# Two passes instead of three for two narrow projections of a hybrid encoder step

## The chip, the cores and the metric

The kernel runs on one core of a Trainium2 chip. The metric is the device time of one execution in microseconds, as the median of several runs. The engines are named as in the profile: PE multiplies matrices, PEld is its weight loading, ACT, DVE and POOL are the three engines that work on elements, and SP issues the DMA transfers.

## The reference, cut to what matters

The program is one inference step of a trunk with two layers, for 1,024 prompt frames and 32 sample frames that share the weights. Each layer normalises its input, projects it, mixes, and projects back. Two of the projected parts are very narrow: the step sizes `dt_raw` of the first layer (16 columns, one for each head) and the forget logits `f_logit` of the second (8 columns).

```python
h = rmsnorm(x, g_pre)
proj = jnp.einsum('bld,de->ble', h, w_in)
u, v, za, zb, xbc, dt_raw = jnp.split(proj, EVEN_SPLITS, axis=-1)   # even layer
dt = jax.nn.softplus(dt_raw.astype(jnp.float32) + dt_bias.astype(jnp.float32))
...
q, k, v, z, f_logit = jnp.split(proj, ODD_SPLITS, axis=-1)          # odd layer
logf = jax.nn.log_sigmoid(f_logit.astype(jnp.float32))
f_cum = jnp.cumsum(jnp.concatenate([past_logf.astype(jnp.float32), logf], axis=1), axis=1)
```

## The kernel before

All 1,056 frames (`TOK`) are handled together, in three chunks of 352 columns (`CH`). The normalised input stands turned in SBUF, features in the partitions, in eight slices of 128 (`k`), and as two numbers for each element: a rounded high part `HH` and the rest `HL`. A weight tile is 128 output columns wide. SP loads it into `WRAW` (two slots, taken in turn), ACT copies it with rounding into `WH` (`split_high`), and POOL subtracts to get the rest `WL` (`split_low`). PE then makes three products for each slice and chunk, high by high, low by high and high by low, into one bank, `PB[c]`: 24 multiplications for a chunk, 72 for a tile. ACT reads each chunk out.

The order on every engine is written out by hand and semaphores tie the engines together. `w_high` and `w_low` count the tiles that ACT and POOL have split; SP may load the next tile into a slot once `w_low` says that the old one was split; `c_read0` to `c_read2` count the chunks that ACT has read out of a bank; `p_chunk` counts chunks that PE has finished.

The tile numbers name the places that matter here. `W_BC[0]` (0) and `W_DT` (1) are the first two tiles; PE works on them in turns (`first_step`), with the turning of `XS` into `HH` and `HL` between them (`x_turn`, three turnings for each slice, through a ring of three banks that ACT and DVE empty). `W_DT` has only 16 real columns, and the other 112 are zeros. Then come `W_BC[1]` to `W_BC[3]`. Behind chunk 0 of `W_BC[1]`, nine turnings bring `DTRAW` (the step sizes) into the frames' order, and DVE and ACT compute on them until PE needs `DTA` for the running sums.

At the border of the two layers the order on PE is: `W_F` (93, 8 real columns) chunks 0 and 1, then chunk 0 of the value tile V, the turning of the sample rows, of row tile 6, chunk 1 of V, the turning of row tile 7, chunk 2 of `W_F`, chunk 2 of V, the nine turnings of `FRAW` (the logits), and chunk 0 of the gate tile Z. A running sum over the logits (`INC`, by a scan on DVE) must be there before PE goes on (`sum_forget`). SP's loads stand in one line: `W_F`, V, Z, then the rows `XT` of tile 7 again, and behind `h1_lo` (17 counts: the second layer's input is complete) the cached logits and the tiles Q and K.

Of the kernel before, what the change touches and what calls it, by code (L numbers as in the profile page):

```python
# [101 lines left out]
def hybrid_trunk(nc, x_prompt, x_sample, cache_k, cache_v, cache_logf, state_ssd, state_conv,  # L102
# [103 lines left out]
    r = Region(A_R5 + 4 * TOK * 4, A_W)  # L206
    DTRAW = r("DTRAW", [HEADS_B, 9 * P])
    DTX, DTN, DTE, DTW, DTL, DTC, DTA, DTD = [r(f"DT{n}", [P, 9, HEADS_B]) for n in "XNEWLCAD"]
# [70 lines left out]
    r = Region(A_R5 + 4 * TOK * 4, A_W)  # L279
    FRAW = r("FRAW", [HEADS_C, 9 * P])  # L280
    FX, FN, FE, FW, FL, FC = [r(f"F{n}", [P, 9, HEADS_C]) for n in ("X", "N", "E", "W", "L", "C")]
# [337 lines left out]
    def _(pool):  # L619
        order = Order(pool, S("pool_order"))  # L620

        def split_low(w):
            pool.wait_ge(S("w_high"), times(w, 1, 1))
            if not isinstance(w[2], int) or w[0] + w[1] * w[2] >= 2:
                pool.wait_ge(S("p_chunk"), times(w, 3, -3))
            pool.tensor_tensor(WL[:, slot(w), :, :], WRAW[:, slot(w), :, :], WH[:, slot(w), :, :].bitcast(f32),  # L626
                               ALU.subtract).then_inc(S("w_low"), 1)

        def split_lows(ws):
            for w in ws:  # L630
                split_low(w)
# [12 lines left out]
        for w in range(W_XZ + 4):  # L644
            split_low(tile_no(w, 1, 0))

# [28 lines left out]
        for u in range(2, OE_UNITS):  # L675
# [3 lines left out]
                               WHS[SLOT3[u % 3]][:, HALF:D].bitcast(f32), ALU.subtract).then_inc(S("w_low"), 1)  # L679
        split_low(tile_no(W_F, 1, 0))  # L680
        split_low(tile_no(W_QKVZ + V_, 4, 0))
# [75 lines left out]
    def _(pe):  # L757
# [11 lines left out]

        def project_chunk(w, u, c, hi, lo, start=True, stop=True, ready=None, ks=range(KT)):  # L770

            if c == 0:
                pe.wait_ge(S("w_low"), times(w, 1, 1))
            if start and not (isinstance(u[2], int) and u[0] + u[1] * u[2] == 0):
                pe.wait_ge(S(f"c_read{c}"), times(u, 1, 0))
            cols = slice(c * CH, (c + 1) * CH)
            for k in ks:
                if ready and len(ready) == 2:
                    pe.wait_ge(S(ready[k % 2]), c * 4 + k // 2 + 1)
                elif ready and (c == 0 or len(ks) < KT):  # L780
                    pe.wait_ge(S(ready[0]), k + 1)
                wh, wl = WH[:, slot(w), k, :], WL[:, slot(w), k, :]
                mm(PB[c][:, 0:CH], wh, hi[:, k, cols], start=start and k == 0, stop=False)
                mm(PB[c][:, 0:CH], wh, lo[:, k, cols], start=False, stop=False)
                last = mm(PB[c][:, 0:CH], wl, hi[:, k, cols], start=False, stop=stop and k == KT - 1)
            if ks[-1] == KT - 1:
                last.then_inc(S("p_chunk"), 1)
# [27 lines left out]
        def first_step(w, c, bank, k):  # L815

            if k == 0:
                pe.wait_ge(S("w_low"), w + 1)
            pe.wait_ge(S("h_lo"), c * KT + k + 1)
            cols = slice(c * CH, (c + 1) * CH)  # L820
            mm(PB[bank][:, 0:CH], WH[:, w, k, :], HH[:, k, cols], start=k == 0, stop=False)
            mm(PB[bank][:, 0:CH], WH[:, w, k, :], HL[:, k, cols], start=False, stop=False)
            last = mm(PB[bank][:, 0:CH], WL[:, w, k, :], HH[:, k, cols], start=False, stop=k == KT - 1)
            if k == KT - 1:
                last.then_inc(S("p_chunk"), 1)
# [28 lines left out]
        for b in range(NB + 1):  # L854
            last = turn(PB[3][:, b * HEADS_B:(b + 1) * HEADS_B], DTRAW[:, b * P:(b + 1) * P])
        last.then_inc(S("dt_turn"), 1)
# [240 lines left out]
        pe.wait_ge(S("h1_lo"), 12)  # L1097
        project_chunk(w_f, u_f, 0, HH, HL)
        project_chunk(w_f, u_f, 1, HH, HL)
        project_chunk(w_v, u_v, 0, HH, HL)  # L1100
# [7 lines left out]
        pe.wait_ge(S("h1_lo"), 17)  # L1108
        project_chunk(w_f, u_f, 2, HH, HL)
        def turn_forget():  # L1110

            pe.wait_ge(S("fc"), 1)
            pe.wait_ge(S("c_read2"), W_F - OE_UNITS + 1)
            for b in range(NB + 1):
                last = turn(PB[3][:, b * HEADS_C:(b + 1) * HEADS_C], FRAW[:, b * P:(b + 1) * P])
            last.then_inc(S("lt_turn"), 1)
# [214 lines left out]
    def _(act):  # L1331
# [106 lines left out]

        raw = whole(DTRAW, HEADS_B)
        for c in range(3):  # L1440
            read_first(c, parted(XR, 3, SAMP), c, 2 * c + 1)
            if c == 2:
                act.wait_ge(S("w_raw0"), loads_of_slot(tile_no(W_BC[1], 1, 0)))
                copy(WH[:, 0, :, :], WRAW[:, 0, :, :]).then_inc(S("w_high"), 1)
            read_first((7, 6, 5)[c], raw, c, 2 * c + 2, HEADS_B)
        split_high(tile_no(W_BC[2], 1, 0))
# [271 lines left out]
        def read_f(c):  # L1718
            act.wait_ge(S("p_chunk"), 3 * W_F + (1, 2, 5)[c])
            copy(FRAW[:, c * CH:(c + 1) * CH], PB[c][0:HEADS_C, 0:CH]).then_inc(S(f"c_read{c}"), 1)  # L1720

# [198 lines left out]
    def _(dve):  # L1920
# [653 lines left out]
```

## Time and profile before

| what | us |
|---|---|
| median of 3 runs (lowest, highest) | 1576.73 (1575.45, 1576.91) |
| time of the profiled execution | 1575.49 |
| its span, first to last instruction | 1573.8 |
| PE busy | 1534.6 (98%) |
| DVE, ACT, POOL busy | 794.0, 677.1, 444.7 |

### The profile page before, as it was taken

The page shows a single profiled execution, that of the slowest core. Times are in us where ns is not written, and L with a number is a line of the kernel's source. Part 1 is how long each engine was busy: PE and PEld are TensorE (multiplying, and loading weights), DVE is VectorE, ACT ScalarE, POOL GpSimd, SP SyncE. Part 2 cuts the span into 40 slices and gives each one's busy share as a digit, 9 for nine tenths or more (in the row PEclk, how much of TensorE's full clock was granted, in tenths as well). Part 3 has the DMA queues.
Part 4 walks back from the last instruction along what each step waited for, and adds up shares of the span by engine and source line. Part 5 has one row for each costly group of instructions (what it writes and reads, how often), then busy time and mean ns, then how long its engine had stood idle before and what let it go on. Part 6 is the DMA issues. An engine that isn't in the chain of part 4 may idle for free.

```text
span 1573.8 us, 26349 instructions
## 1 busy us (share of the span) xinstructions
PE 1534.6 (98%) x9472; PEld 1415.8 (90%) x9472; DVE 794.0 (50%) x1751; ACT 677.1 (43%) x1258; POOL 444.7 (28%) x268
## 2 busy tenths in 40 slices
PE   6999999999999999999999999999999999999998
PEld 5999999999999999988888898999999999988776
DVE  5546777676884231436475243444344343435432
ACT  6444443433233322335455344445454545455321
POOL 1214453553221111344343221222222231215000
PEclk9999999999999999999999999999999999999999
DMA  5122223213102111254456536614241423213121
GB/s 154 43 70 61 74 62 101 60 45 86 53 27 57 41 40 40 79 175 160 153 192 145 56 75 53 68 37 74 37 71 44 71 41 63 61 44 141 55 98 70
DMA packets 129510, 121.09 MB, mean 77 GB/s; under 512 B 10290, under 2 KB 113292, under 8 KB 129452
## 3 DMA queue, kind: packets, MB, share of 16 engines
q1 hardware_dynamic: 129452, 120.32, 31.5%
q8 instruction: 37, 0.61, 0.2%
q14 instruction: 21, 0.17, 0.0%
HBM read 101.64 MB, written 18.66 MB: 76 GB/s over the span
## 4 chain that ended last, share of the span: by engine, by line
PE 88%; ACT 4%; DVE 3%; issue 3%; DMA 1%; POOL 1%; SPq 0%; ACTq 0%; DVEq 0%; POOLq 0%
PE PB L759 83%; PE PB L763 5%; DMA XT<-in_x_prompt_dram 1%; ACT L1339 1%; ACT L1804 1%; ACT SB L1893 0%; ACT SQJ L1373 0%; DVE XT L1931 0%; DMA WOR<-in_w_out_odd_dram 0%; DVE SB L1928 0%; ACT WH L1333 0%; POOL WL L626 0%; DMA XS<-in_x_prompt_dram 0%; DVE XS L1928 0%; DVE M L1931 0%
## 5 line engine op out<-in xcount | busy, mean ns | idle before, releaser
L759 PE MATMUL PB<-HH,WH 128*128 128x352 f32 x1872 | 617.5, 330 | 2.5 <-DVE HL L1924 1.6
L759 PE MATMUL PB<-HH,WL 128*128 128x352 f32 x1872 | 601.9, 322 | 0.0
L759 PE MATMUL PB<-HL,WH 128*128 128x352 f32 x1872 | 601.1, 321 | 0.0
L759 PEld LDWEIGHTS PB<-HH,WH 128*128 128x128 f32 x1872 | 351.9, 188 | 17.5 <-issue 10.4
L759 PEld LDWEIGHTS PB<-HL,WH 128*128 128x128 f32 x1872 | 352.9, 189 | 0.2
L759 PEld LDWEIGHTS PB<-HH,WL 128*128 128x128 f32 x1872 | 351.9, 188 | 0.0
L626 POOL TENSOR_TENSOR WL<-WRAW,WH 128x1024 fp32r<-128x1024 f32 x81 | 199.9, 2468 | 534.3 <-ACT WH L1333 527.6
L1333 ACT ACTIVATE WH<-WRAW 128x1024 fp32r<-128x1024 f32 x112 | 118.0, 1054 | 14.3 <-DMA WRAW<-in_w_out_even_dram 6.1
L1893 ACT ACTIVATE SB<-SB,small 128x128 f32<-128x128 f32 (+8 forms) x72 | 53.8, 748 | 78.6 <-DVE small L1928 78.6
L1924 DVE TENSOR_TENSOR Y<-PB,Y 128x128 f32 (+3 forms) x72 | 20.2, 281 | 127.6 <-PE PB L759 127.5
L759 PE MATMUL PB<-PT,VTOK 128*128 128x128 f32 (+2 forms) x624 | 81.5, 274 | 0.0
L759 PEld LDWEIGHTS PB<-PT,VTOK 128*128 128x128 f32 (+1 forms) x624 | 78.3, 191 | 1.5
L759 PE MATMUL PB<-KALL,QT 128*128 128x512 f32 (+4 forms) x208 | 78.0, 482 | 0.0
L654 POOL TENSOR_TENSOR M<-M,CBT 128x512 f32<-128x512 f32 (+1 forms) x48 | 62.2, 1324 | 47.5 <-ACT M L1522 47.5
L759 PE MATMUL PB<-WH,YSH 128*128 128x512 f32 x192 | 75.1, 391 | 0.0
L759 PE MATMUL PB<-WL,YSH 128*128 128x512 f32 x192 | 74.7, 389 | 0.0
L1333 ACT ACTIVATE PT<-PB 128x512 f32<-128x512 f32 (+3 forms) x112 | 45.9, 447 | 61.2 <-PE PB L763 61.1
L678 POOL TENSOR_TENSOR WL<-WRAW,WH 128x512 fp32r<-128x512 f32 x30 | 53.5, 1784 | 63.6 <-ACT WH L1333 63.6
L759 PE MATMUL PB<-WH,YSL 128*128 128x512 f32 x172 | 66.9, 389 | 0.0
L1924 DVE TENSOR_TENSOR UG<-UG,ZG 128x1056 f32<-128x1056 f32 x8 | 12.2, 1528 | 105.6 <-ACT ZG L1353 105.6
L2442 DVE CUSTOM_DVE_ANT_0 SB<-PB,NFB 128x512 f32<-128x512 f32 (+4 forms) x104 | 54.5, 547 | 21.4 <-issue 14.4
L704 POOL TENSOR_TENSOR NRM<-QT 128x352 f32<-128x352 f32 x24 | 20.0, 832 | 147.9 <-ACT QT L1333 147.9
(312 smaller groups left out, 2362.6 us busy)
## 6 DMA issues: line engine op xcount, KB each, us to landing
WRAW<-in_w_out_even_dram SPq DMA_DIRECT2D x48, 512.0 KB, 3.6
WRAW<-in_w_in_even_dram SPq DMA_DIRECT2D x44, 512.0 KB, 3.8
WRAW<-in_w_in_odd_dram SPq DMA_DIRECT2D x32, 512.0 KB, 8.2
ACSB<-acs_rows SPq DMA_DIRECT2D x16, 528.0 KB, 5.3
NFB<-nf_rows SPq DMA_DIRECT2D x8, 656.0 KB, 3.9
XS<-in_x_prompt_dram SPq DMA_DIRECT2D x8, 512.0 KB, 6.2
XT<-in_x_prompt_dram SPq DMA_DIRECT2D x8, 512.0 KB, 5.3
x_rows<-OG SPq DMA_DIRECT2D x8, 512.0 KB, 5.4
```

The lines of the kernel that those rows point to most:

```text
L626: pool.tensor_tensor(WL[:, slot(w), :, :], WRAW[:, slot(w), :, :], WH[:, slot(w), :, :].bitcast(f32), ALU.subtract).then_inc(S("w_low"), 1)
L654: pool.tensor_tensor(m, m, CBT[0:rows, g, b0:b0 + nb, 0:rows], ALU.mult).then_inc(S("m"), 1)
L678: pool.tensor_tensor(WLS[SLOT3[u % 3]][:, HALF:D], raw[:, HALF:D], WHS[SLOT3[u % 3]][:, HALF:D].bitcast(f32), ALU.subtract).then_inc(S("w_ ...
L704: last = pool.tensor_tensor(NRM[:, n, cols], src, src, ALU.mult)
L759: return pe.matmul(out, lhsT, rhs, start=start, stop=stop)
L763: return pe.transpose(out, in_, IDENT[0:n, 0:n])
L1333: return act.activation(out, in_, ACT.Copy, scale=scale)
L1339: act.add_instruction(mybir.InstLoadActFuncSet(name=nc.get_next_instruction_name(), act_func_set_id=LN_EXP_SET, ins=[], outs=[]))
L1804: act.activation(Y1[:, p, :], Y1[:, p, :], ACT.Silu).then_inc(S("zs"), 1)
L1893: act.activation(SB[0:rows, 0:width], SB[0:rows, 0:width], ACT.Exp, scale=SCALE, bias=NBIAS[0:rows, :], accum_out=RSUM[0:rows, :]).then_in ...
L1924: return dve.tensor_tensor(out, a, b, op)
L2442: order(dve.tensor_tensor_reduce(SB[0:rows, c0:c1], PB[3 + k][0:rows, 0:c1 - c0], NFB[0:rows, key0 + c0:key0 + c1], 1.0, -3.0e38, ALU.add, ...
```

## The change

In the two narrow tiles the low parts of the weights are put into the columns beside the high ones: columns 16 to 31 of `WH` for `W_DT`, columns 8 to 15 for `W_F` (`stack_low` on POOL, for 128 and 64 elements of each partition, in place of 1,024). PE then needs two passes, with `HH` and with `HL`, and not a third with `WL`. The projection comes out with twice the rows, the high weights' part above the low weights' part, and ACT copies 32 or 16 rows. The two halves are added when they are turned: in place of a turning against the identity, PE multiplies with `STACKB` or `STACKC`, two identities on top of each other, which DVE makes once.

```diff
+        def stack_low(w, heads):
+            pool.wait_ge(S("w_high"), times(w, 1, 1))
+            pool.tensor_tensor(WH[:, slot(w), :, heads:2 * heads], WRAW[:, slot(w), :, 0:heads],
+                               WH[:, slot(w), :, 0:heads].bitcast(f32), ALU.subtract).then_inc(S("w_low"), 1)
...
         for w in range(W_XZ + 4):
-            split_low(tile_no(w, 1, 0))
+            if w == W_DT:
+                stack_low(tile_no(w, 1, 0), HEADS_B)
+            else:
+                split_low(tile_no(w, 1, 0))
...
-        split_low(tile_no(W_F, 1, 0))
+        stack_low(tile_no(W_F, 1, 0), HEADS_C)
         split_low(tile_no(W_QKVZ + V_, 4, 0))
...
                 mm(PB[c][:, 0:CH], wh, hi[:, k, cols], start=start and k == 0, stop=False)
-                mm(PB[c][:, 0:CH], wh, lo[:, k, cols], start=False, stop=False)
-                last = mm(PB[c][:, 0:CH], wl, hi[:, k, cols], start=False, stop=stop and k == KT - 1)
+                end = stop and k == KT - 1
+                last = mm(PB[c][:, 0:CH], wh, lo[:, k, cols], start=False, stop=stacked and end)
+                if not stacked:
+                    last = mm(PB[c][:, 0:CH], wl, hi[:, k, cols], start=False, stop=end)
...
-            last = mm(PB[bank][:, 0:CH], WL[:, w, k, :], HH[:, k, cols], start=False, stop=k == KT - 1)
+            if w != W_DT:
+                last = mm(PB[bank][:, 0:CH], WL[:, w, k, :], HH[:, k, cols], start=False, stop=k == KT - 1)
...
-            last = turn(PB[3][:, b * HEADS_B:(b + 1) * HEADS_B], DTRAW[:, b * P:(b + 1) * P])
+            last = mm(PB[3][:, b * HEADS_B:(b + 1) * HEADS_B], DTRAW[:, b * P:(b + 1) * P], STACKB[:, :])
...
-                last = turn(PB[3][:, b * HEADS_C:(b + 1) * HEADS_C], FRAW[:, b * P:(b + 1) * P])
+                last = mm(PB[3][:, b * HEADS_C:(b + 1) * HEADS_C], FRAW[:, b * P:(b + 1) * P], STACKC[:, :])
...
+        for stack, heads in ((STACKB, HEADS_B), (STACKC, HEADS_C)):
+            order(tt(stack[:, :], IDENT[0:2 * heads, 0:heads], IDENT[0:2 * heads, heads:2 * heads], ALU.add))
+        order.fence()
         dve.memset(DTRAW[:, TOK:], 0.0).then_inc(S("dtc"), 1)
```

On PE, the end of chunk 2 of `W_DT` and the first multiplications of `W_BC[1]` read like this before:

```order
L759 MATMUL PB<-HH,WH 128x352 [waits h_lo]
L759 MATMUL PB<-HL,WH 128x352
L759 MATMUL PB<-HH,WL 128x352
L759 MATMUL PB<-HH,WH 128x352 [waits h_lo]
L759 MATMUL PB<-HL,WH 128x352
L759 MATMUL PB<-HH,WL 128x352
L759 MATMUL PB<-HH,WH 128x352 [waits c_read0,w_low]
L759 MATMUL PB<-HL,WH 128x352
```

and like this in the changed kernel:

```order
L769 MATMUL PB<-HH,WH 128x352 [waits h_lo]
L769 MATMUL PB<-HL,WH 128x352
L769 MATMUL PB<-HH,WH 128x352 [waits h_lo]
L769 MATMUL PB<-HL,WH 128x352
L769 MATMUL PB<-HH,WH 128x352 [waits h_lo]
L769 MATMUL PB<-HL,WH 128x352
L769 MATMUL PB<-HH,WH 128x352 [waits c_read0,w_low]
L769 MATMUL PB<-HL,WH 128x352
L769 MATMUL PB<-HH,WL 128x352
```

Each slice of `W_DT` has lost its third multiplication, and the wait for `w_low` of `W_BC[1]` now stands behind 16 multiplications of the chunk and not 24.

On PE, the place where `DTRAW` is turned, behind chunk 0 of `W_BC[1]`, reads like this before:

```order
L759 MATMUL PB<-HL,WH 128x352
L759 MATMUL PB<-HH,WL 128x352
L763 MATMUL PB<-IDENT,DTRAW 128x16 [waits dtc,c_read2]
L763 MATMUL PB<-IDENT,DTRAW 128x16 x8
L759 MATMUL PB<-HH,WH 128x352 [waits c_read1]
```

and like this in the changed kernel:

```order
L769 MATMUL PB<-HL,WH 128x352
L769 MATMUL PB<-HH,WL 128x352
L769 MATMUL PB<-STACKB,DTRAW 128x16 [waits dtc,c_read2]
L769 MATMUL PB<-STACKB,DTRAW 128x16 x8
L769 MATMUL PB<-HH,WH 128x352 [waits c_read1]
```

Nothing has moved, but the nine turnings are plain products of 32-bit numbers. The nine of `FRAW` change in the same way.

On POOL, the splits at the border of the layers (`WLC` is the last tile of the first layer's output projection, then follow `W_F` and V) read like this before:

```order
L678 TENSOR_TENSOR WLC<-WRAW,WHC 128x512 [waits w_high]
L626 TENSOR_TENSOR WL<-WRAW,WH 128x1024 [waits p_chunk,w_high] x2
L683 CAST IDENTB<-IDENT 128x128 [waits h1_lo]
L684 MEMSET MASKD 128x128
L687 AFFINE_SELECT MASKD<-MASKD 128x128 [waits pool_order]
```

and like this in the changed kernel:

```order
L688 TENSOR_TENSOR WLC<-WRAW,WHC 128x512 [waits w_high]
L633 TENSOR_TENSOR WH<-WRAW,WH 128x8x8 [waits w_high]
L628 TENSOR_TENSOR WL<-WRAW,WH 128x1024 [waits p_chunk,w_high]
L693 CAST IDENTB<-IDENT 128x128 [waits h1_lo]
L694 MEMSET MASKD 128x128
```

The split of `W_F` is smaller and no longer waits for `p_chunk`, that is, for PE to have finished with the slot of `WL`. SP's load of tile Z, which waits for `w_low` of `W_F`, and the load of `XT` behind it can go out earlier.

## Rows read from the trace of the kernel before

**Rows 1.** The page, the chain that ended last, shares by engine.

```profile
PE 88%; ACT 4%; DVE 3%; issue 3%; DMA 1%; POOL 1%; SPq 0%; ACTq 0%; DVEq 0%; POOLq 0%
```

**Rows 2.** Timeline of PE: first, last multiplication of chunk 2 of `W_DT`, then `W_BC[1]`.

```profile
start us, us, engine line op out<-in xcount [idle before <-releaser]
...
49.56 0.32 PE L759 MATMUL PB<-HH,WH 128*128 128x352 f32 x1
...
53.22 0.32 PE L759 MATMUL PB<-HH,WL 128*128 128x352 f32 x1
53.79 0.43 PE L759 MATMUL PB<-HH,WH 128*128 128x352 f32 x1 [0.25 <-POOL WL L626]
```

**Rows 3.** Timeline of PE: first, fourth turning beside `W_DT` chunk 0; first beside `W_BC[0]` chunk 1.

```profile
27.55 0.49 PE L763 MATMUL PB<-IDENT,XS 128*128 128x128 f32 x3
...
30.55 0.55 PE L763 MATMUL PB<-IDENT,XS 128*128 128x128 f32 x3 [0.39 <-DVE HL L1931]
...
35.24 0.55 PE L763 MATMUL PB<-IDENT,XS 128*128 128x128 f32 x3
```

**Rows 4.** Timeline of DVE: the last normalised rows, those of the sample.

```profile
33.91 0.74 DVE L1928 TENSOR_SCALAR XS<-XS,small 32x1024 f32<-32x1024 f32 x1
```

**Rows 5.** Timeline of ACT: first read behind chunk 2 of `W_BC[0]`.

```profile
49.76 0.53 ACT L1333 ACTIVATE XR<-PB 128x320 f32<-128x320 f32 x2 [3.36 <-PE PB L759]
```

**Rows 6.** Timeline of PE: the nine turnings of `DTRAW` and what follows them.

```profile
57.85 0.73 PE L763 MATMUL PB<-IDENT,DTRAW 16*128 16x16 f32 x9
58.50 0.43 PE L759 MATMUL PB<-HH,WH 128*128 128x352 f32 x1
```

**Rows 7.** Timeline of PE: `sum_forget`, two and four small products, and what follows.

```profile
887.38 0.43 PE L759 MATMUL PB<-LT,TRIF 128*128 128x88 f32 x2 [1.63 <-DVE INC L2393]
887.64 0.55 PE L759 MATMUL PB<-INC,ONES 128*128 128x56 f32 x4
888.04 0.41 PE L759 MATMUL PB<-HH,WH 128*128 128x352 f32 x1
```

**Rows 8.** Timelines of DVE and PE: `DTA`, and the running sums over it.

```profile
65.95 0.31 DVE L1924 TENSOR_TENSOR DTA<-TOKQ,EALB 128x144 f32<-128x144 f32 x1
...
66.32 0.51 PE L759 MATMUL PB<-DTA,TRI 128*128 128x144 f32 x2
```

**Rows 9.** Timelines of ACT, POOL and PE: V is split, and its chunk 0 starts.

```profile
854.65 1.05 ACT L1333 ACTIVATE WH<-WRAW 128x1024 fp32r<-128x1024 f32 x1
...
855.77 3.39 POOL L626 TENSOR_TENSOR WL<-WRAW,WH 128x1024 fp32r<-128x1024 f32 x1 [4.51 <-ACT WH L1333]
...
859.22 0.43 PE L759 MATMUL PB<-HH,WH 128*128 128x352 f32 x1
```

**Rows 10.** The chain that ended last: rows `XT` of tile 7, issue to landing.

```profile
851.71 9.84 DMA XT<-in_x_prompt_dram
```

**Rows 11.** Timelines of PE and ACT: tile 6 turned, `FRAW` chunk 1 read, chunk 1 of V.

```profile
864.92 1.06 PE L763 MATMUL PB<-IDENT,XT 128*128 128x128 f32 x8 [1.00 <-DVE XT L1931]
...
865.27 0.44 ACT L1333 ACTIVATE FRAW<-PB 8x352 f32<-8x352 f32 x1
...
865.76 0.43 PE L759 MATMUL PB<-HH,WH 128*128 128x352 f32 x1
```

**Rows 12.** Timelines of PE and SP: chunk 2 of `W_F`; Q's load issued, and its time to landing.

```profile
872.29 0.43 PE L759 MATMUL PB<-HH,WH 128*128 128x352 f32 x1 [1.57 <-DVE HL L1924]
...
872.69 0.47 SPq L367 DMA_DIRECT2D WRAW<-in_w_in_odd_dram  x1
...
DMA to landing us min/median/max: 8.7/8.7/8.7
```

**Rows 13.** Timelines of ACT, POOL and DVE: Q is split, and `FW` of the logits.

```profile
881.49 1.05 ACT L1333 ACTIVATE WH<-WRAW 128x1024 fp32r<-128x1024 f32 x1
...
882.61 2.38 POOL L626 TENSOR_TENSOR WL<-WRAW,WH 128x1024 fp32r<-128x1024 f32 x1 [2.32 <-ACT WH L1333]
...
882.84 2.21 DVE L1928 TENSOR_SCALAR FW<-FE 128x72 f32<-128x72 f32 x1 [0.33 <-ACT FE L1839]
```

**Rows 14.** Issue of V's load (842.2) and its time to landing.

```profile
DMA to landing us min/median/max: 7.7/7.7/7.7
```

More of the change, by code:

```diff
@@ L159, in hybrid_trunk @@
     DCOL = const("DCOL", [P, 8])
+    STACKB = const("STACKB", [2 * HEADS_B, HEADS_B])
+    STACKC = const("STACKC", [2 * HEADS_C, HEADS_C])
     small = const("small", [P, 64])
@@ L206, in hybrid_trunk @@
     r = Region(A_R5 + 4 * TOK * 4, A_W)
-    DTRAW = r("DTRAW", [HEADS_B, 9 * P])
+    DTRAW = r("DTRAW", [2 * HEADS_B, 9 * P])
     DTX, DTN, DTE, DTW, DTL, DTC, DTA, DTD = [r(f"DT{n}", [P, 9, HEADS_B]) for n in "XNEWLCAD"]
@@ L279, in hybrid_trunk @@
     r = Region(A_R5 + 4 * TOK * 4, A_W)
-    FRAW = r("FRAW", [HEADS_C, 9 * P])
+    FRAW = r("FRAW", [2 * HEADS_C, 9 * P])
     FX, FN, FE, FW, FL, FC = [r(f"F{n}", [P, 9, HEADS_C]) for n in ("X", "N", "E", "W", "L", "C")]
@@ L768, in key_wait, with project_chunk @@
                 pe.wait_ge(S("masks"), 1)
-        def project_chunk(w, u, c, hi, lo, start=True, stop=True, ready=None, ks=range(KT)):
+        def project_chunk(w, u, c, hi, lo, start=True, stop=True, ready=None, ks=range(KT),
+                          stacked=False):
             if c == 0:
@@ L821, in first_step @@
             mm(PB[bank][:, 0:CH], WH[:, w, k, :], HH[:, k, cols], start=k == 0, stop=False)
-            mm(PB[bank][:, 0:CH], WH[:, w, k, :], HL[:, k, cols], start=False, stop=False)
-            last = mm(PB[bank][:, 0:CH], WL[:, w, k, :], HH[:, k, cols], start=False, stop=k == KT - 1)
+            last = mm(PB[bank][:, 0:CH], WH[:, w, k, :], HL[:, k, cols], start=False,
+                      stop=w == W_DT and k == KT - 1)
+            if w != W_DT:
+                last = mm(PB[bank][:, 0:CH], WL[:, w, k, :], HH[:, k, cols], start=False, stop=k == KT - 1)
             if k == KT - 1:
@@ L1097, in _ @@
         pe.wait_ge(S("h1_lo"), 12)
-        project_chunk(w_f, u_f, 0, HH, HL)
-        project_chunk(w_f, u_f, 1, HH, HL)
+        project_chunk(w_f, u_f, 0, HH, HL, stacked=True)
+        project_chunk(w_f, u_f, 1, HH, HL, stacked=True)
         project_chunk(w_v, u_v, 0, HH, HL)
@@ L1108, in _ @@
         pe.wait_ge(S("h1_lo"), 17)
-        project_chunk(w_f, u_f, 2, HH, HL)
+        project_chunk(w_f, u_f, 2, HH, HL, stacked=True)
         def turn_forget():
@@ L1437, in read_first @@
             last.then_inc(S(f"c_read{c}"), 1)
-        raw = whole(DTRAW, HEADS_B)
+        raw = whole(DTRAW, 2 * HEADS_B)
         for c in range(3):
@@ L1444, in _ @@
                 copy(WH[:, 0, :, :], WRAW[:, 0, :, :]).then_inc(S("w_high"), 1)
-            read_first((7, 6, 5)[c], raw, c, 2 * c + 2, HEADS_B)
+            read_first((7, 6, 5)[c], raw, c, 2 * c + 2, 2 * HEADS_B)
         split_high(tile_no(W_BC[2], 1, 0))
@@ L1719, in read_f @@
             act.wait_ge(S("p_chunk"), 3 * W_F + (1, 2, 5)[c])
-            copy(FRAW[:, c * CH:(c + 1) * CH], PB[c][0:HEADS_C, 0:CH]).then_inc(S(f"c_read{c}"), 1)
+            copy(FRAW[:, c * CH:(c + 1) * CH], PB[c][0:2 * HEADS_C, 0:CH]).then_inc(S(f"c_read{c}"), 1)
         squares(SMP)
```

## The prediction

> **What bounds the kernel now.** I read the page first, then the chain that ended last, then the timelines of the two places that the change touches. The page gives PE 88% of the chain [rows 1], so PE's own work is the time nearly everywhere, and a multiplication taken off PE is worth its pace as long as PE doesn't wait next for something that has not become earlier. The pace: 24 multiplications of a chunk start from 49.56 to 53.22 [rows 2], 3.66 us for 23 steps, 0.159 us each. The change removes 48 of them, 24 in each layer, so 7.63 us is the most there is. The timelines then show where PE, just behind each removed piece, stands or would stand waiting for POOL, ACT, DVE or a transfer. That decides the sum, so I go through both places in order of time. Beyond them PE has hardly a gap and the loads are released by its own progress, so I carry an earlier start through to the end.
>
> **First place, W_DT.** The change there, piece by piece:
>
> Chunk 0. The first four slices are mixed with turnings. The fourth group of turnings starts at 30.55, after a wait of 0.39 us for DVE's `HL` [rows 3]. That wait goes back to a turning before 27.55 and to ACT and DVE work behind it, which holds no multiplication of `W_DT`. So the three removed before 30.55 only lengthen the wait: nothing. Five remain (slices 3 to 7): 5 x 0.159 = 0.80 us. The next turnings then are ready at 35.24 - 0.80 = 34.44, but they need the sample rows, which DVE ends at 33.91 + 0.74 = 34.65 [rows 3, 4]. With the 0.05 us from such an end to PE's start, 34.70: the gain is 0.54 us.
>
> Chunk 1. No wait is recorded in it, and DVE's ring has room: 8 x 0.159 = 1.27 us. Sum 1.81 us.
>
> Chunk 2. Here is the first loss. `W_BC[1]` can't start before its weights are split, and that split begins only when chunk 2 of `W_BC[0]` is done: ACT reads that chunk at 49.76, rounds the tile, POOL subtracts, and PE starts at 53.79 having waited 0.25 us for POOL [rows 2, 5]. All of this moves by 1.81 us with the chunk that starts it, to 51.98. Chunk 2 of `W_DT` is what PE does meanwhile. It gets 8 x 0.159 = 1.27 us shorter, and PE waits 1.27 us longer. Gain still 1.81 us.
>
> The turning. Nine turnings take 58.50 - 57.85 = 0.65 us [rows 6]. A plain product of 32-bit numbers shows as two instructions. Six small ones take 888.04 - 887.38 = 0.66 us, 0.11 each [rows 7]. Nine products are 18 instructions, 1.98 us, 1.33 us more than before. The ends: at the turnings' own pace (0.65 / 9 = 0.072) 18 cost 1.30 us, 0.65 more; at the most that the wider pair of the running sums leaves (0.51 us for two with their tail [rows 8]) 18 cost 4.6 us, 3.9 more. I take 0.11, since those rows are as narrow. Would it be hidden? PE reaches the running sums at 66.32 just when `DTA` is there (65.95 + 0.31 = 66.26 [rows 8]). `DTA` hangs on the convolution that begins with the read of rows 5, so it moves 1.81 us, and PE arrives later than it: nothing hides the 1.33 us. First place: 1.81 - 1.33 = 0.48 us gained, between 1.16 gained and 2.1 lost.
>
> The Trainium skill speaks against this step twice. "Perfetto Trace Analysis", section Transposes, wants a transposition done as one and not as an ordinary product, and rows 6 and 7 have that sign. "TensorE: Matmul & The Clock Gate", section LDWEIGHTS, prices a weight load by its columns alone, 128 columns over 1.2, or 107 ns; by it my estimate would be 18 x 0.107 = 1.93 us, and the sum would gain 0.05 us. The turnings load 128 columns too and pass at 0.072 us, so as a rule for every load it doesn't hold here.
>
> The rest is free. The two additions for the stacks and the larger clear stand on DVE between the last `HL` and the convolution, where it is idle until the read of rows 5. ACT's copies have twice the partitions and the same columns. POOL's smaller split is not waited for by PE.
>
> **Second place, W_F.** Chunks 0 and 1 lose 16 multiplications, 2.54 us. But V's chunk 0 starts at 859.22, and POOL's split of V ends at 855.77 + 3.39 = 859.16; that split begins when ACT, after squares of rows and a root chain, rounds V at 854.65 [rows 9]. None of it waits for `W_F`'s products. PE waits 2.5 us in their place. Gain 0.
>
> Then SP. `w_low` of `W_F` came at about 851.3 and let SP issue Z and, behind it, `XT`, which landed 9.84 us after 851.71 and held the chain [rows 10]. Now POOL's small split waits only for ACT's rounding, and `XT` can be issued and lands some us earlier. PE's wait of 1.00 us before tile 6 is turned goes away [rows 11]. But V's chunk 1 also needs its bank, and ACT reads `FRAW` out of that bank only at 865.27 + 0.44 = 865.71, behind the squares of row tile 7 and behind the sample rows, which PE turns after V's chunk 0; PE starts chunk 1 at 865.76, 0.05 us later [rows 11]. So two releases tie, and removing one gives nothing: gain 0, with 1.0 us as the bound if I misread the tie.
>
> Chunk 2 of `W_F` starts at 872.29 when `h1_lo` is complete [rows 12], unmoved, and is 8 x 0.159 = 1.27 us shorter. V's chunk 2 and the turnings follow that much earlier. What then holds PE is `INC`, for which it waits 1.63 us until 887.38 [rows 7]. `INC` hangs on `FW`, which DVE holds for 2.21 us, until 882.84 + 2.21 = 885.05, just when POOL ends its split of Q at 882.61 + 2.38 = 884.99. POOL starts after ACT rounds Q at 881.49 [rows 13]. And ACT can't do that before Q has landed: 872.69 + 8.7 = 881.4 [rows 12]. Q's load waits for `h1_lo`, unmoved. So `INC` stays, and the 1.27 us turn into waiting. The nine dearer products of `FRAW` (1.33 us) fit into the 1.63 + 1.27 us of wait. Second place: 0.
>
> **Sum.** 0.48 + 0 = 0.5 us. The profiled execution took 1575.49 us (span 1573.8 and 1.7 around it) and would take 1575.0. The median of the runs shown is 1576.73, 1.24 us above it, so 1576.2. About 0.2%, 3.2 us, is what a measurement of this kernel can tell from no change; this is far inside it. Most of the 7.63 us of removed PE work becomes waiting: 0.48 + 0.26 in chunk 0, 1.27 in chunk 2, 3.81 at the border.
>
> **Rivals.**
>
> (a) The border does open. If the bank's read is not what holds V's chunk 1, the 1.00 us comes through, `h1_lo` and Q's load move by it, and `INC` with them. With the cheaper end of the turning (0.65 instead of 1.33) the gain is 0.48 + 1.0 + 0.68 = 2.2 us: 1574.5. For it: the recorded wait is put down to DVE alone. Against it: 865.71 and 865.76.
>
> (b) The work simply goes: PE's share of 88% as it stands. 48 x 0.159 - 2 x 1.33 = 5.0 us, 1571.7. It needs all four waits to be something else than I read them. Against it: each ends within 0.1 us of PE's start.
>
> (c) Slower: V comes late. Z and `XT` now go out while V's load is on its way (issued 842.2, 7.7 us to landing, so 849.9 [rows 14]). If the transfers shared the engines, V could land as the last of the three, later by up to the 9.84 us that Z and `XT` took together [rows 10]: 859.7. ACT wants V at 854.65 [rows 9]; that is the point from which it costs. 859.7 - 854.65 = 5.1 us, less 0.5: 1581.3, slower by 0.3%. Against it: rows in one queue that I read land in the order of their issue.
>
> (d) The stacked turning is at its dear end, 3.9 us more at the first place: 1576.7 + 2.1 = 1578.8. At the second place the excess of about 1 us over the waits would come on top if the logits got late.
>
> **How the numbers follow.** Forecast (between 1.5 us gained and 1.5 lost) 0.66; (a) 0.16; (b) 0.08; (c) 0.05; (d) 0.05. Faster by over 0.2% takes (b) and a little of (a): 0.09. Slower takes half of (c) and a little of (d): 0.04. The rest, 0.87, is the same. The range leaves out (b) and (c): from (a), less 0.7 us, half the spread of the three runs shown, 1573.8, to 1578.3, short of (d).
>
> **What the changed profile would show.** PE waits about 1.5 us for POOL before `W_BC[1]`, which starts near 52.0; 18 instructions on `STACKB` in about 2.0 us; the running sums near 65.8. PE waits about 2.5 us before V's chunk 0 at 859.2 less 0.5 (the carried gain), and `XT` no longer stands in the chain. Before `sum_forget` PE waits some 1.6 us or more. I am wrong if V's chunk 1 comes much earlier than ACT's second read of `FRAW` did, if `FW` is not held by POOL, or if a product with the stack costs over 0.3 us.

## The result: 7.5 us slower, and most of it in code that the change doesn't touch

The changed kernel takes 1583.26 us (5 runs, 1582.13 to 1584.09) against 1575.81 us of the kernel before (5 runs, 1575.19 to 1576.91): ratio 1.0043, 95% interval 1.0032 to 1.0054. I had forecast 1576.2 and a range up to 1578.3. The profiled execution has a span of 1581.3 us, 7.5 us more than before.

The page's row for PE, with the counts of its instructions:

```profile
PE 1539.0 (97%) x9442; PEld 1414.7 (89%) x9442; DVE 788.4 (50%) x1753; ACT 677.3 (43%) x1258; POOL 440.8 (28%) x268
```

PE has 30 instructions fewer than before (48 multiplications gone, 9 turnings replaced by 18 instructions at each of two places), and yet is busy for 1539.0 us where it was 1534.6. So this is not waiting alone: work that is left has become slower.

Where the 7.5 us come from is read from the starts of the same piece of work in the two traces:

| piece of work | before | after | difference |
|---|---|---|---|
| `W_BC[1]` chunk 0 starts [rows 2] | 53.79 | 51.87 | -1.92 |
| first multiplication behind the nine turnings [rows 6] | 58.50 | 58.03 | -0.47 |
| running sums over `DTA` [rows 8] | 66.3 | 67.4 | +1.1 |
| output projection of the first layer, first multiplication | 655.43 | 656.26 | +0.83 |
| the same, last multiplication | 851.05 | 857.31 | +6.26 |
| V chunk 0 [rows 9] | 859.22 | 865.27 | +6.05 |
| `sum_forget` [rows 7] | 887.38 | 893.51 | +6.13 |
| the turning of `NFT` behind it | 891.98 | 899.66 | +7.68 |
| span | 1573.8 | 1581.3 | +7.5 |

Three steps stand out: 5.4 us in the output projection, and twice 1.5 us just behind a place of the change (58 to 67 us, and 893 to 900 us). I call such a difference between the two traces, in the start of the same piece of work, the drift.

**First place.** Timeline of PE in the changed kernel: the start of `W_BC[1]`, the products with `STACKB`, and what follows them.

```profile
start us, us, engine line op out<-in xcount [idle before <-releaser]
51.87 0.43 PE L769 MATMUL PB<-HH,WH 128*128 128x352 f32 x1 [1.48 <-POOL WL L628]
...
55.93 2.18 PE L769 MATMUL PB<-STACKB,DTRAW 32*128 32x16 f32 x18
58.03 0.43 PE L769 MATMUL PB<-HH,WH 128*128 128x352 f32 x1
58.30 0.41 PE L769 MATMUL PB<-HL,WH 128*128 128x352 f32 x1
58.50 0.49 PE L769 MATMUL PB<-HH,WL 128*128 128x352 f32 x1
58.80 0.49 PE L769 MATMUL PB<-HH,WH 128*128 128x352 f32 x1
...
61.44 0.49 PE L769 MATMUL PB<-HH,WH 128*128 128x352 f32 x1
61.73 0.36 PE L769 MATMUL PB<-HL,WH 128*128 128x352 f32 x1
```

The wait of 1.5 us for POOL and the start at 51.87 are as forecast. The eighteen product instructions hold PE for 58.03 - 55.93 = 2.10 us. Behind them the multiplications start 0.29 us apart instead of 0.159, for 3.4 us. The windows give the granted clock (the column behind POOL, 1.00 being 2.4 GHz; a stretch wholly at 1.2 GHz shows 0.50); the kernel before has 1.00 in all of these:

```profile
core 0: us, PE busy (x) PEld busy (x) DVE busy (x) ACT busy (x) POOL busy (x), PEclk, DMA share, GB/s
58.00:60.00 2.00, 2.00 (x9) 1.97 (x10) 0.00 (x0) 1.98 (x3) 0.00 (x0) 0.60 0.19 57
60.00:62.00 2.00, 2.00 (x9) 2.00 (x9) 1.10 (x6) 1.08 (x4) 0.00 (x0) 0.55 0.00 0
62.00:64.00 2.00, 2.00 (x14) 2.00 (x13) 1.66 (x6) 0.91 (x3) 0.00 (x0) 1.00 0.00 0
...
895.00:900.00 5.00, 5.00 (x25) 4.96 (x24) 0.00 (x0) 0.14 (x1) 0.00 (x0) 0.69 0.40 43
```

**Output projection.** Timeline of PE in the middle of this stage, two rows 27 multiplications apart:

```profile
699.60 0.40 PE L769 MATMUL PB<-WL,YSH 128*128 128x512 f32 x1
...
705.92 0.39 PE L769 MATMUL PB<-WLC,YSHD 128*128 128x512 f32 x1
```

That is 6.32 / 27 = 0.234 us each. In the kernel before, two rows of the same stage, again 27 multiplications apart, give 6.12 / 27 = 0.227 us each:

```profile
699.76 0.39 PE L759 MATMUL PB<-WH,YSH 128*128 128x512 f32 x1
...
705.88 0.39 PE L759 MATMUL PB<-WH,YSH 128*128 128x512 f32 x1
```

No wait is recorded and the clock is 1.00 in both. The groups by form say the same, with the duration of one in ns behind the comma. The kernel before, then the changed one:

```profile
L759 PE MATMUL PB<-WH,YSH 128*128 128x512 f32 x180 | 70.3, 391 | 0.0
...
L759 PE MATMUL PB<-WHC,YSHD 128*128 128x512 f32 x90 | 35.3, 392 | 0.0
```

```profile
L769 PE MATMUL PB<-WH,YSH 128*128 128x512 f32 x179 | 71.2, 398 | 0.0
...
L769 PE MATMUL PB<-WHC,YSHD 128*128 128x512 f32 x84 | 33.6, 400 | 0.0
```

**Border.** Timelines of POOL, PE and DVE from `W_F` to `sum_forget`:

```profile
851.44 0.32 POOL L633 TENSOR_TENSOR WH<-WRAW,WH 128x64 fp32r<-128x64 f32 x1 [3.42 <-ACT WH L1348]
...
865.27 0.43 PE L769 MATMUL PB<-HH,WH 128*128 128x352 f32 x1 [2.44 <-POOL WL L628]
871.84 0.43 PE L769 MATMUL PB<-HH,WH 128*128 128x352 f32 x1 [0.82 <-ACT FRAW L1348]
878.37 0.43 PE L769 MATMUL PB<-HH,WH 128*128 128x352 f32 x1 [1.57 <-DVE HL L1939]
...
885.86 2.17 PE L769 MATMUL PB<-STACKC,FRAW 16*128 16x8 f32 x18
...
889.14 2.05 DVE L1943 TENSOR_SCALAR FW<-FE 128x72 f32<-128x72 f32 x1 [0.33 <-ACT FE L1854]
...
893.51 0.43 PE L769 MATMUL PB<-LT,TRIF 128*128 128x88 f32 x2 [1.47 <-DVE INC L2411]
```

Here nearly every wait is the one forecast: 2.44 us for POOL's `WL` before V's chunk 0; before V's chunk 1 no longer DVE's `XT` but 0.82 us for ACT's read of `FRAW`, the second of the two tied releases; `FW` at the end of POOL's split, and the wait for `INC`. The drift is the same before and behind these waits.

### The profile page after: what moved, and what is told of

Same layout as the page of the kernel before. It is cut to its first block and busy times, and to the rows that moved or that the text cites. A ratio compares the mean times of both kernels' runs of the same rounds, so it can differ in the third digit from the quotient of the medians.

```text
span 1581.3 us, 26290 instructions
## 1 busy us (share of the span) xinstructions
PE 1539.0 (97%) x9442; PEld 1414.7 (89%) x9442; DVE 788.4 (50%) x1753; ACT 677.3 (43%) x1258; POOL 440.8 (28%) x268
## 5 line engine op out<-in xcount | busy, mean ns | idle before, releaser
L769 PE MATMUL PB<-HH,WL 128*128 128x352 f32 x1824 | 587.8, 322 | 0.0
L769 PEld LDWEIGHTS PB<-HH,WL 128*128 128x128 f32 x1824 | 344.2, 189 | 0.0
L628 POOL TENSOR_TENSOR WL<-WRAW,WH 128x1024 fp32r<-128x1024 f32 x79 | 194.4, 2460 | 530.9 <-ACT WH L1348 530.8
```

Of the source, the lines that this page charges most:

```text
L769: return pe.matmul(out, lhsT, rhs, start=start, stop=stop)
```

## The experiments

Each chip that ran experiments also ran the kernel before. All ratios are against those runs. Expectations are quoted in the words on record.

| run | us | before | ratio (95% interval) | drift in its trace at 640, 855 and 900 us |
|---|---|---|---|---|
| e1_pad96 | 1582.00 | 1576.84 | 1.0035 (1.0021, 1.0049) | 0.0, +5.3, +5.4 |
| e2_unshifted | 1577.41 | 1576.84 | 1.0003 (0.9994, 1.0012) | +0.9, +1.1, +2.6 |
| e3_turned_halves | 1575.34 | 1576.84 | 0.9990 (0.9981, 0.9999) | -1.4, -1.4, +1.7 |
| e4_products_only | 1578.15 | 1576.84 | 1.0014 (1.0005, 1.0023) | +1.0, +1.0, +2.2 |
| e5_pad64 | 1582.12 | 1576.61 | 1.0030 (1.0020, 1.0040) | +0.5, +4.8, +6.4 |
| e6_whc_off | 1577.96 | 1576.61 | 1.0006 (0.9996, 1.0015) | -0.2, +2.1, +2.1 |
| e7_ysh_off | 1580.11 | 1576.61 | 1.0020 (1.0010, 1.0030) | -0.4, +3.6, +5.2 |
| e8_dt_turned_wait_hidden | 1575.92 | 1576.61 | 0.9993 (0.9984, 1.0002) | +0.3, +0.3, +0.5 |
| e9_dt_turned | 1575.97 | 1576.37 | 0.9995 (0.9986, 1.0004) | -0.9, -0.5, +1.3 |
| e10_f_turned | 1578.18 | 1576.37 | 1.0014 (1.0005, 1.0023) | +0.4, +0.4, +2.2 |
| e11_dt_sums_later | 1573.37 | 1576.37 | 0.9980 (0.9971, 0.9989) | -3.3, -3.2, -1.6 |
| e12_minus128 | 1581.42 | 1576.37 | 1.0028 (1.0018, 1.0039) | +0.1, +4.7, +6.3 |
| e13_all_on96 | 1577.03 | 1576.02 | 1.0004 (0.9994, 1.0013) | +0.2, +0.3, +0.4 |
| e14_all_but | 1581.48 | 1576.02 | 1.0030 (1.0019, 1.0042) | -0.1, +4.5, +6.1 |
| e15_swapped | 1575.74 | 1576.02 | 1.0000 (0.9990, 1.0010) | -0.2, +0.3, +0.3 |
| e16_before_again | 1578.13 | 1576.02 | 1.0012 (1.0001, 1.0022) | -0.6, -0.5, +1.1 |
| e17_products_no_wait | 1576.67 | 1576.34 | 0.9994 (0.9985, 1.0004) | -0.5, -0.5, +1.4 |
| e18_unshifted_again | 1578.42 | 1576.34 | 1.0006 (0.9996, 1.0016) | +1.3, +1.1, +3.2 |

The last column compares the profiled execution with that of the kernel before: the start of the same instruction of ACT, behind 640, 855 and 900 us, in the one less that in the other. It tells where in the kernel something changes, to about half a microsecond (e16 is the kernel before itself and stands at -0.6 and -0.5). The medians tell less: e16 still comes out at 1.0012, so 0.1% in the ratio is no evidence, and the runs of the kernel before on one chip lie 3 to 7 us apart. Much of that goes with the clock: on e9's chip its 15 runs with a mean granted clock of 0.999 average 1575.8 us, the 4 with 0.997 average 1577.8.

### Where the tiles lie

**e1**, the kernel before with unused memory in the place of the two stacks:

```diff
+    PAD = const("PAD", [P, 24])
     small = const("small", [P, 64])
```

> The kernel before with 96 unused bytes of each partition put where STACKB and STACKC stand in the change; no instruction differs. Theory A (the tiles behind the constants, YSH, YSL, WHC and WLC of the first layer's output projection among them, are slower 96 bytes further on): the 512-column multiplications start every 234 ns instead of 226.7 in that stage, about +5.1 us, so 1581 us, and no dip of the clock at 58 or 894 us. Rival B (the slower pace comes from the change's instructions or its clock, not from addresses): within 1 us of the kernel before.

The first theory held: nothing changes up to 640 us, and the output projection alone takes 5.3 us more, at the changed kernel's pace (its one fall of the clock, at 1506 us, is counted further down):

```profile
L760 PE MATMUL PB<-WH,YSH 128*128 128x512 f32 x180 | 71.7, 398 | 0.0
...
L760 PE MATMUL PB<-WHC,YSHD 128*128 128x512 f32 x85 | 34.0, 400 | 0.0
```

**e2**, the changed kernel with the stacks in free room elsewhere:

```diff
-    STACKB = const("STACKB", [2 * HEADS_B, HEADS_B])
-    STACKC = const("STACKC", [2 * HEADS_C, HEADS_C])
+    STACKC = small[0:2 * HEADS_C, 56:64]
...
     ACSS = r("ACSS", [HEADS_B, DEC])
+    STACKB = r("STACKB", [2 * HEADS_B, HEADS_B])
```

> The changed kernel with STACKC in eight unused columns of small and STACKB in unused room behind ACSS, so that every other tile has its address of before. Theory A: the output projection is back at 226.7 ns, 5.1 us less than the change, about 1578.2 us, 2.4 us over the kernel before, the rest being the two dips of the clock (1.5 us each) and the products (+1.45) less the 1.9 us gained in front. Rival B: as the change, 1583.3 us.

The pace is back (0.2 us lost in the whole stage), and the time falls to 1577.41. So the two stacks cost 5 us by the room that they take, whatever is in them.

Which tiles, and by what rule? **e5** took 64 bytes for the 96; **e6** moved `WHC` and `WLC` alone by 96; **e7** moved `YSH` and `YSL` by 32 and `WHC` and `WLC` by 64; **e12** moved all four 128 bytes back.

> The kernel before with 64 unused bytes in front of small instead of 96. The tiles behind the constants start at a multiple of 128 bytes before, 32 bytes off a multiple of 64 with the 96. Theory A1 (what matters is whether the tiles start at a multiple of 64 bytes): pace 226.7 ns in the output projection, no change within 1 us. Rival A2 (any shift, or one off a multiple of 128, does it): 234 ns, +5 us.

> The kernel before with WHC and WLC alone 96 bytes further on; they are the streamed operand of every third unit of the output projection. If the loss comes from each multiplication that touches a shifted tile: WHC,YSHD and WLC,YSHD pairs at 232 to 235 ns, the others at 226.7, +1.7 us. If only the shifted YSH and YSL do it: no change.

> The kernel before with YSH and YSL 32 bytes further on (off a multiple of 64) and WHC and WLC 64 bytes further on (at a multiple of 64): YSH and YSL are the loaded weights of two of every three units. Each multiplication that touches a shifted tile: the WH,YSH and WL,YSH pairs at 234 ns, the WHC,YSHD pairs at 226.7, +3.4 us. If only WHC and WLC do it: no change.

> The kernel before with the tiles behind the constants moved by 128 bytes (towards lower addresses), the place made by moving DCOL and seven small columns to the end of memory. 96 bytes and 64 bytes on cost 5.3 and 4.8 us. Theory (the output projection is slow when the tiles of its operands don't start at a multiple of 128 bytes): pace 226.7 ns, same time as before within 1 us. Rival (any move from the layout of before does it): 231 to 235 ns, +4.5 to +5.5 us.

Of e6 first, then of e7, the groups by form between 640 and 840 us (before: 391 and 392 ns):

```profile
L759 PE MATMUL PB<-WH,YSH 128*128 128x512 f32 x180 | 70.5, 392 | 0.0
...
L759 PE MATMUL PB<-WHC,YSHD 128*128 128x512 f32 x89 | 35.4, 397 | 0.0
```

```profile
L759 PE MATMUL PB<-WH,YSH 128*128 128x512 f32 x180 | 71.5, 397 | 0.0
...
L759 PE MATMUL PB<-WHC,YSHD 128*128 128x512 f32 x87 | 34.5, 396 | 0.0
...
L759 PE MATMUL PB<-WHC,YSLD 128*128 128x512 f32 x79 | 30.8, 389 | 0.0
```

The products that touch a moved tile are the slow ones; e6 cost 2.3 us where I expected 1.7, e7 4.0 where I expected 3.4. But both rules that I had for the address fell: with 64 bytes and with 128 bytes the stage loses 4.4 and 4.6 us (396 ns and 396 ns for `WH,YSH`). So I asked whether the place counts, or the place against the other operand. **e13** moves the whole layout by 96 bytes; **e14** moves everything up to the constants by 128 and leaves the four tiles; **e15** exchanges `WHC` and `WLC`, 4,096 bytes apart:

```diff
-    base = (nc.sbuf_base + 63) // 64 * 64
+    base = (nc.sbuf_base + 63) // 64 * 64 + 96
```

> The kernel before with its whole layout 96 bytes further on, so that no tile moves against another. Theory R (the place of the operands against one another matters): pace 226.9 ns in the output projection, as before within 1 us. Theory S (the place as such matters): 231 to 234 ns there, +4.5 to +5.5 us, and perhaps more in other stages.

> Everything up to the constants 128 bytes further on, the tiles behind the constants (YSH, YSL, WHC, WLC) where they were: by distance the same as the run with these tiles 128 bytes back. Theory R: 233 ns, about +4.7 us. Theory S: 226.9 ns, no change, unless WH, WL and YSHD are slowed by their own move.

> The kernel before with WHC and WLC in one another's place (4,096 bytes apart), nothing else moved. If only the low bits of an address or of a distance matter: 226.9 ns, as before. If the layout of before is one lucky case among moves of any size: WHC and WLC pairs at 231 to 235 ns, +1.5 to +2 us.

Of e13, then of e14, one group each:

```profile
L759 PE MATMUL PB<-WH,YSH 128*128 128x512 f32 x180 | 70.3, 391 | 0.0
```

```profile
L760 PE MATMUL PB<-WH,YSH 128*128 128x512 f32 x180 | 71.3, 396 | 0.0
```

Theory R held: it is the distance between the tiles. With all of them moved together by the 96 bytes that cost 5.3 us in e1, nothing is lost; with the others moved and these four left where they were, 4.6 us are; and the exchange of e15, by 4,096 bytes, costs nothing. In the layout before, `WH` starts at byte 196,736 and is read with `YSH` at 214,912, 71 times 256 bytes on; `WHC`, at 221,056, is read with `YSHD` at 149,632, 279 times 256 bytes apart; and the tiles and their parts are multiples of 256 long. The nine layouts fit "fast at a multiple of 256 bytes, slow at 32, 64, 96 or 128 off one" but for one pair: `WHC,YSLD` in e7 is 64 off and keeps its 389 ns (in e5, at the same distance, it has 394). So the distance between its own two tiles doesn't decide alone what a multiplication loses. No run tried a tile moved by exactly 256, so the 256 is a fit and not shown. Nor did any run move both tiles of a pair together against the rest, so that it is the two operands of one multiplication, and not a moved tile against something else that is read or written meanwhile, is argued from e6 and e7 and not shown. Why distance matters is open.

### The products and the clock

**e3** has two passes as the change, real turnings of 32 (16) rows, and DVE adds the halves. **e4** is the kernel before with plain products against `IDENT` in place of the turnings.

```diff
-            last = mm(PB[3][:, b * HEADS_B:(b + 1) * HEADS_B], DTRAW[:, b * P:(b + 1) * P], STACKB[:, :])
+            last = turn(PB[3][:, b * 2 * HEADS_B:(b + 1) * 2 * HEADS_B], DTRAW[:, b * P:(b + 1) * P])
```

> Two passes as in the change, no stacks: the nine turnings of 32 (16) rows are real turnings into 288 (144) columns of the bank and DVE adds the two halves; addresses as in the kernel before. If the dips of the clock belong to the small products: both gone, the nine turnings at 0.65 us as before, so 1.9 us gained in front and kept, 0 to 0.3 at the border, about 1573.9 us (1.9 faster than before). Rival (the dips belong to the waits that the missing third pass leaves, 1.5 us for POOL's WL in front and the later wait for INC): the clock still falls at 58 us, 1.5 us given back there, and perhaps at 894 us, so 1575.4 to 1577 us.

> The kernel before with only the nine turnings at each place replaced by plain products against the identity; three passes, same addresses. Products cost 2.1 us for 0.65 at each place, +1.45 in front; at the border the wait for DVE and INC behind them shows whether it hides. If the clock falls for the small products alone: +1.5 us more at each place, in all about +3 to +5 us, 1579 to 1581 us. Rival (the dip needs the wait ahead of it as well, which this kernel has only at 0.25 us): +1.45 to +2.9 us without a dip, 1577.3 to 1578.7 us.

In front (up to 100 us) e3 is as its first theory has it: the nine wider turnings take 0.67 us, about that of [rows 6], the clock stays at 1.00 from 54 to 66 us, and 1.4 us are kept to the border. e4 pays its 1.5 us for the products and shows no fall at 58 us, so at that point it looked as if a fall needed the wait of 1.5 us and the products together. **e17** (products, but `WL`'s multiplications last, so that nothing waits for POOL) and **e18** (e2 once more) asked for that:

> The changed kernel with STACKB and STACKC where no tile moves, chunk 0 of W_BC[1] with its WL multiplications last (so no wait for POOL) and the sums of DTA one chunk later. If the fall of the clock at 58 us needs the wait and the products together: full clock from 50 to 80 us, drift about -3.2 + 1.45 = -1.75 us at 100 us, and 1.3 to 2.4 us faster than before less what the border's two-pass W_F and its clock take (up to 1.7). Rival (the products do it by themselves, and the run with products only escaped by chance): half clock behind the products, drift -0.3 us at 100 us.

> The changed kernel with the stacks where no tile moves, once more, for its trace. If the products behind the wait make the clock fall each time: some ten to twelve multiplications at 0.293 us from 58 us on, +1.5 us. If it comes and goes as at 889 us: it may be missing here.

Windows of e17, where the products begin at 54 us:

```profile
54.00:56.00 2.00, 2.00 (x19) 1.78 (x17) 2.00 (x1) 0.00 (x0) 1.31 (x1) 1.00 0.63 185
56.00:58.00 2.00, 2.00 (x11) 1.97 (x11) 1.75 (x2) 0.18 (x1) 0.00 (x0) 0.69 0.73 193
58.00:60.00 2.00, 2.00 (x8) 2.00 (x7) 0.00 (x0) 1.98 (x3) 0.00 (x0) 0.50 0.24 72
```

The rival came true: no wait ahead, and still the clock falls to the lower level. Counted over the traces: the clock falls behind these products in 4 of 5 (the changed kernel, e2, e17, e18; not e4), and in none of the 15 that turn there. The same holds at the border: the clock falls with the end of the eighteen products of `FRAW`, ahead of the wait for `INC`, in 3 of 5 traces (e4, e17, e18), and behind the turnings of `FRAW` in none of 15. Of e4, whose products end at 884.18:

```profile
880.00:885.00 5.00, 5.00 (x35) 4.76 (x34) 0.68 (x2) 1.42 (x2) 2.65 (x2) 0.91 0.75 89
885.00:890.00 5.00, 5.00 (x27) 5.00 (x26) 3.30 (x11) 0.97 (x4) 1.02 (x1) 0.75 1.01 126
```

With 7 falls behind 10 stretches of products and none behind 30 of turnings, that the small products bring the clock down is as good as shown; why not each time isn't. At the border this fall costs little, since it shortens the wait for `INC` (0.29 us are left of it in e17 and e18). And without the moved tiles the change as a whole gains or loses nothing that the medians can tell: 1.0003 and 1.0006 (e2, e18).

### The border

**e9** is e3 with the step sizes alone in two passes, **e10** is e3 with `W_F` alone in two passes.

> As the run with both halves turned, but two passes for the step sizes alone; W_F and the border as before. If the front's gain is only lost at the border when W_F changes the waits there: 1.4 to 1.8 us gained in front, none lost at 855 to 892 us, about 1.5 us faster than the kernel before. Rival (the border takes it back whatever W_F does): 0 to 0.5 us faster.

> Two passes for W_F alone, its nine turnings real ones with the halves added on DVE; the front as before. If the border's loss belongs to the two-pass W_F: drift 0 up to 855 us, then one or two stretches of half clock between 857 and 892 us, +1.3 to +3 us in the profile. Rival (it came from arriving there early): within 0.3 us of the kernel before, no dip.

**e16** is the kernel before once more, for a second trace.

> The kernel before once more, for its trace. If the fall of the clock at 885 to 895 us comes and goes from one execution to the next whatever the kernel: it may stand here too, and the span is then 1.2 to 1.6 us above 1573.8. If it belongs to the changed kernels: all of 500 to 1573 us at the full clock.

e10 shows the border without anything else. Timeline of its PE:

```profile
859.58 0.43 PE L764 MATMUL PB<-HH,WH 128*128 128x352 f32 x1 [2.59 <-POOL WL L626]
...
880.23 0.73 PE L768 MATMUL PB<-IDENT,FRAW 16*128 16x16 f32 x9
...
887.98 0.43 PE L764 MATMUL PB<-LT,TRIF 128*128 128x88 f32 x2 [2.98 <-DVE INC L2404]
```

The removed work has become waiting: 2.59 us for `WL`, and 2.98 us for `INC` where before it was 1.63. The place gains nothing. What it loses is clock: its trace has half clock from 889 us on. But so has e16, the kernel before, in its windows:

```profile
885.00:889.00 4.00, 2.42 (x17) 2.16 (x16) 1.71 (x8) 0.67 (x2) 0.00 (x0) 0.98 0.98 148
889.00:892.00 3.00, 3.00 (x12) 3.00 (x12) 0.00 (x0) 0.00 (x0) 0.00 (x0) 0.50 0.52 51
```

So the fall behind `INC` is not the change's: of the 13 traces with the old border 7 have it, each at +1.5 to +1.8 us, and the one that I had read before predicting was one of the 6 without. Of the six traces with two passes of `W_F` four wait 1.4 us or more for `INC`, and three of these have the fall behind it (the changed kernel, e3, e10; not e2). In e17 and e18 hardly any of that wait is left, and the fall there is the one with the products of `FRAW`.

What does come with two passes of `W_F` is a fall at the start of V's chunk 0, right behind the wait for `WL`: it stands in 4 of the 6 (e2, e3, e17, e18), and in none of the 14 traces that don't wait there. Windows of e2, where V's chunk 0 starts at 860.29 after 2.59 us of waiting:

```profile
855.00:860.00 5.00, 2.70 (x17) 2.40 (x16) 3.52 (x7) 4.66 (x13) 3.09 (x1) 1.00 0.47 168
860.00:865.00 5.00, 4.71 (x20) 4.71 (x21) 3.85 (x4) 0.61 (x3) 0.24 (x1) 0.66 0.29 119
```

e3's trace has both falls and loses its gain to them, but it is the slowest of e3's 11 runs (1577.23 us, mean clock 0.996; 8 of the 11 have 0.998 and average 1575.2), and by its median e3 is 1.5 us faster than the kernel before, near the forecast 1.9. e10's 1.0014 is hardly more than e16's 1.0012. e9's expectation of no loss at the border fell, since its trace has the fall behind `INC`, as half of those with the old border have. Two traces of the old border, e1 and e5, have one more fall at 1506 to 1508 us, far from the change, behind a wait of 1.57 us for ACT.

### Hiding the wait for WL

**e8** is e9 with `W_BC[1]`'s chunk 0 reordered, `WL` last; **e11** also takes the running sums one chunk later.

```diff
+        for k in range(KT):
+            mm(PB[0][:, 0:CH], WH[:, slot(w1), k, :], HH[:, k, 0:CH], start=k == 0, stop=False)
+            mm(PB[0][:, 0:CH], WH[:, slot(w1), k, :], HL[:, k, 0:CH], start=False, stop=False)
+        pe.wait_ge(S("w_low"), times(w1, 1, 1))
+        for k in range(KT):
+            last = mm(PB[0][:, 0:CH], WL[:, slot(w1), k, :], HH[:, k, 0:CH], start=False, stop=k == KT - 1)
...
+        w2 = tile_no(W_BC[2], 1, 0)
+        project_chunk(w2, w2, 0, HH, HL)
         pe.wait_ge(S("dtc"), 4)
```

> Two passes for the step sizes alone, W_F as before; addresses as before; the nine turnings are real ones of 32 rows with the halves added on DVE; and chunk 0 of W_BC[1] runs its sixteen multiplications with WH first and the eight with WL last, so that POOL's 2.4 us lie beside them. Front: the third pass of all three chunks is gone, 3.8 us less less at most 0.3 that is left of the wait for ACT's WH: -2.9 to -3.5 us at the start of chunk 1, no dip of the clock at 58 us, and kept to the end, since the border is that of before: about 1572.3 to 1573 us where the kernel before has 1575.8. Rival (PE runs into another wait in front, or the clock falls at the border as it did for the two-pass W_F): half or less of it is left, 1574.5 us or more.

> As the run with the wait for WL hidden, and the running sums of DTA and the turning of TOKQ each one chunk of W_BC[2] later on PE, so that DVE's chain for DTA (ready at 65.9 us) lies beside chunk 0 of W_BC[2]. If the earlier run lost its gain to the wait for DTA and to the clock's fall behind it: no wait for DTA, no half clock at 66 us, 2.7 to 3.3 us gained and kept, about 1573 us where the kernel before has 1575.8 to 1576.6. Rival (the next wait, for TOKQ's copy or for a bank that ACT reads later, takes it): 1 us or more of new waits between 66 and 80 us, gain under 2 us.

e8 hides the wait and gains nothing: `DTA` is ready at 64.97 us, where e9 has it at 65.13, since the read that DVE's convolution ahead of it begins with is no earlier either (48.12 and 48.31), and PE now stands there, with the clock down behind it. Timeline, then windows:

```profile
65.03 0.57 PE L767 MATMUL PB<-DTA,TRI 128*128 128x144 f32 x2 [1.98 <-DVE DTA L1945]
```

```profile
64.00:66.00 2.00, 0.97 (x5) 0.97 (x6) 0.90 (x3) 1.24 (x3) 0.68 (x1) 0.84 0.00 0
66.00:68.00 2.00, 2.00 (x9) 2.00 (x8) 1.26 (x5) 1.20 (x4) 1.69 (x1) 0.50 0.00 0
```

With a chunk of `W_BC[2]` ahead of the sums (e11) this wait is gone too, and 3.2 us are kept up to 855 us, as expected; behind `INC` its trace has the fall of the old border. Its median of 1573.37 is 3.0 us below the kernel before on the same chip; it is the only kernel here that is faster beyond what e16 leaves in doubt.

## Why the prediction was wrong

- **Failed: "Beyond them PE has hardly a gap ... so I carry an earlier start through to the end."** I took it that stages whose code is unchanged keep their pace. The diff places two new tiles in front of others, and by that alone the 832 512-column multiplications that the trace has of the first layer's output projection start 6 to 7 ns further apart each: 5.4 us of the 7.5 (e1 5.3 alone, e2 0.2 with the stacks elsewhere). Nothing in my four rivals had it. Without it the forecast of no change would have stood (e2: 1.0003), but partly by luck, since the fall of the clock below wasn't in the sum.
- **Mis-sized by what follows it: the turning.** Predicted +1.33 us, measured 2.10 - 0.65 = +1.45. But the clock falls behind it, and with that the term is 1.45 + 1.5 = 3.0 us, towards the dear end that I had priced at 3.9 for another reason. That turns the first place from +0.48 gained to 0.8 to 1.1 lost.
- **Right: the first place up to the product.** 1.81 us forecast, 1.92 seen; the wait of 1.5 us for POOL; `WL` of `W_BC[1]` as the loss of chunk 2.
- **Right: the border gives nothing.** 2.44 us (forecast 2.5) for `WL`; the two tied releases before V's chunk 1; `INC` held by `FW`, `FW` by POOL's split. e10 shows it alone: 2.59 and 2.98 us of wait. The products of `FRAW`, 2.1 us, did fit into the wait. Not foreseen was the fall of the clock behind `INC`, 1.5 us of the profile's 7.5; it comes and goes, and belongs to the comparison of two single traces more than to the change. Nor was the one behind the longer wait for `WL`, which 4 of 6 traces with this border have, though not that of the changed kernel.
- **Rivals.** (a), (b): none of the waits opened. (c): V came no later. (d) had the right place, the wrong mechanism. The one on the slower side that happened was missing from the list.

The account of the profile: -1.9 + 1.45 + 1.5 (first place) + 5.4 (distance) + 1.5 (clock at `INC`) = 7.9, less 0.4 in small drifts, against 7.5.

## What to carry to other kernels

A diff that allocates something has a second effect: it moves whatever is allocated behind it. Before predicting, list the tiles that move and, of the stages that read them, the longest; put new constants where nothing moves, or time a version with the padding alone. And a multiplication taken off an engine that is "always busy" is worth something only if the releases behind it move as well: here the gain came (3.0 us) only once the wait for `WL` and the wait for `DTA` behind it were both given work to hide them.

## What the runs showed of the hardware that I had not expected

- A 512-column multiplication in the 32-bit type starts every 227 ns or every 231 to 235 ns, by how far in memory its tiles lie from one another; e1, e13 and e14 separate that from where they lie.
- Eighteen instructions of small products, 2.1 us in all, are followed by 3.4 us at half clock in 4 of 5 traces in front and in 3 of 5 at the border; nine real turnings of 8 to 32 rows by none (15 traces, two places each).
- The wait of 1.6 to 1.8 us for `INC` is followed by half clock in 7 of 13 traces whose border is the same, 1.5 to 1.8 us each time, and in one of the two traces of one and the same kernel (e16 and not before).
- A wait of 2.6 us for `WL` is followed by half clock in 4 of 5 traces (e2, e3, e17, e18; not e10), one of 2.44 us, in the changed kernel, isn't.
